# Composing the pool projection and the pool map into one weight, on one core

## The reference

```python
z = rms_norm(h, norm_gain)
proj = z @ w_in                                   # split into q, k, v, g_attn, u_pool, g_pool
o_attn = chunked_window_attention(rotary(q), rotary(k), v, sinks)
u = u_pool.reshape(L, 4, 256)                     # four channel groups
pooled = trailing_mean(u, window=2, 4, 8, 16) - u # one window for each group
mixed = einsum("lgc,gcd->lgd", pooled, w_pool)    # a 256 x 256 map for each group
o_pool = mixed.reshape(L, 1024) * pool_scale
h = h + concat(silu(g_attn) * o_attn, silu(g_pool) * o_pool) @ w_out
y = rms_norm(h, final_norm_gain)[meta dropped]
```

## Time and profile before

| | |
|---|---|
| median of 3 runs | 1375.55 us (1375.39 to 1375.70) |
| span of the profiled execution (first to last instruction) | 1373.9 us |
| mean granted TensorE clock in it | 0.996 |
| PE busy | 1341.3 us, 98% |
| DVE, ACT, POOL busy | 780.0, 536.5, 189.1 us |
| DMA | 102.25 MB, mean 74 GB/s |

### The profile page before, as it was taken

How to read it: one execution, slowest core, us unless ns; L and a number is a source line. 1 busy time by engine, 2 the same in 40 slices (tenths; PEclk the granted TensorE clock), 3 DMA queues, 4 the chain that set the end, 5 groups by cost and what they waited for, 6 DMA issues and landing times.

```text
span 1373.9 us, 18172 instructions
## 1 busy us (share of the span) xinstructions
PE 1341.3 (98%) x6293; PEld 1105.2 (80%) x6293; DVE 780.0 (57%) x1067; ACT 536.5 (39%) x1218; POOL 189.1 (14%) x252
## 2 busy tenths in 40 slices
PE   8999999999999999999999999999999999999997
PEld 6888888787887877888888888887878787788886
DVE  6435355867677674355366435367676868533635
ACT  7222323544444443235344222334444444322433
POOL 1201012111110101000002101031111111000000
PEclk9999999999999999999999999999999999999999
DMA  6011111010101006534433111100101010333442
GB/s 234 32 61 46 46 46 47 8 49 17 50 19 43 26 22 218 161 118 166 143 108 109 44 61 46 46 31 9 61 8 61 8 61 8 107 125 117 151 164 100
DMA packets 29820, 102.25 MB, mean 74 GB/s; under 512 B 3360, under 2 KB 5440, under 8 KB 29792
## 3 DMA queue, kind: packets, MB, share of 16 engines
q1 hardware_dynamic: 22608, 76.03, 16.4%
q0 software_dynamic: 7184, 25.86, 5.6%
HBM read 93.49 MB, written 8.39 MB: 74 GB/s over the span
## 4 chain that ended last, share of the span: by engine, by line
PE 55%; issue 29%; DVE 12%; ACT 1%; POOL 1%; DMA 1%; DVEq 0%; POOLq 0%; SPq 0%; ACTq 0%
PE ps L1148 9%; PE ps L1149 9%; PE ps L1147 8%; PE ps L945 5%; PE ps L946 5%; PE ps L947 5%; DVE wsum L812 3%; DVE stat L799 2%; DVE stat L802 1%; PE ps L1108 1%; PE ps L1067 1%; PE ps L1069 1%; PE ps L1068 1%; PE ps L1093 1%; PE ps L1109 1%
## 5 line engine op out<-in xcount | busy, mean ns | idle before, releaser
L945 PE MATMUL ps<-zh,wsplit 128*128 128x512 f32 x1072 | 421.9, 394 | 0.1
L946 PE MATMUL ps<-zl,wsplit 128*128 128x512 f32 x1072 | 418.3, 390 | 0.0
L947 PE MATMUL ps<-zh,wsplit 128*128 128x512 f32 x1072 | 417.7, 390 | 0.0
L659 DVE TENSOR_TENSOR wsplit<-wraw,wsplit 128x1024 fp32r<-128x1024 f32 (+1 forms) x148 | 203.2, 1373 | 241.2 <-ACT wsplit L437 241.2
L437 ACT ACTIVATE wsplit<-wraw 128x1024 fp32r<-128x1024 f32 (+1 forms) x148 | 146.3, 988 | 265.6 <-PE ps L1149 223.1
L947 PEld LDWEIGHTS ps<-zh,wsplit 128*128 128x128 f32 x1072 | 201.2, 188 | 43.1
L945 PEld LDWEIGHTS ps<-zh,wsplit 128*128 128x128 f32 x1072 | 201.3, 188 | 41.3 <-DVE wsplit L659 0.6
L946 PEld LDWEIGHTS ps<-zl,wsplit 128*128 128x128 f32 x1072 | 201.4, 188 | 39.1
L1149 PE MATMUL ps<-wsplit,gsl 128*128 128x512 f32 x512 | 203.3, 397 | 0.0
L1148 PE MATMUL ps<-wsplit,gsh 128*128 128x512 f32 x512 | 202.7, 396 | 0.0
L1147 PE MATMUL ps<-wsplit,gsh 128*128 128x512 f32 x512 | 199.4, 390 | 2.3 <-POOL gsl L396 2.0
(11 more groups left out here) (156 smaller groups left out, 1588.5 us busy)
## 6 DMA issues: line engine op xcount, KB each, us to landing
wraw<-in_wo SPq DMA_DIRECT2D x64, 512.0 KB, 3.3
wraw<-in_wa SPq DMA_DIRECT2D x36, 512.0 KB, 3.3
wraw<-in_wb SPq DMA_DIRECT2D x32, 512.0 KB, 3.3
rows<-in_x POOLq DMA_DIRECT2D x16, 512.0 KB, 4.3
xr<-in_x POOLq DMA_DIRECT2D x12, 512.0 KB, 3.9
out_y<-rows POOLq DMA_DIRECT2D x8, 512.0 KB, 5.1
xr<-in_x SPq DMA_DIRECT2D x4, 512.0 KB, 6.2
wraw<-in_wp SPq DMA_DIRECT2D x16, 128.0 KB, 2.0
```

The lines of the kernel that those rows point to most:

```text
L659: ve.tensor_tensor(wl[:, slot, 0:size], wraw[:, slot, 0:size], wh[:, slot, 0:size].bitcast(F32), ALU.subtract).then_inc(w_lo, 1)
L945: te.matmul(ps[:, PB[bank], :], w_h, rhs_z(zh, tb, k), start=k == 0, stop=False)
L946: te.matmul(ps[:, PB[bank], :], w_h, rhs_z(zl, tb, k), start=False, stop=False)
L947: last = te.matmul(ps[:, PB[bank], :], w_l, rhs_z(zh, tb, k), start=False, stop=k == KT - 1)
```

## The change

Projection and map are both linear in the channels and pooling acts along the tokens alone, so the map can be applied to the weight. `kernel` now passes the pool columns of `w_in` turned (`wu`, eight blocks of 128 x 1024) and `w_pool` (four blocks of 128 x 512). At the opening of the first half four products are made, one for each group: 48 matmuls of 128 x 256 into PSUM banks 0 to 3 (`product`); ACT copies them to `cout` (`copy_product`), and POOL writes them to the DRAM scratch `wc`. In stage B blocks 0 and 1 are loaded from `wc`; the trailing mean goes to `pooled`, which needs no splitting; a DVE multiplication of 128 x 1024 into the gates stands at the end of chunks 2 and 3. The pool map is gone: `GROUP_BLOCKS` is 4, not 6.

```diff
         def z_bank(h, t):
+            if h == 0 and t < 4:
+                return 4 + 2 * (t % 2)
             return PB[0] if t == 3 else 2 * (t % 3)
+        def composed(eng):
+            for parity in range(2):
+                eng.wait_ge(wc_out[parity], 16 * 2 * NG // 2)
...
 # SP
+            def load_pool(g):
+                if g >= 2:
+                    sp.wait_ge(cp_lo, g - 1)
+                sp.dma_start(cpraw[:, g % 2, :], wp[g]).then_inc(cp_in[g % 2], 16)
+                for ct in range(2):
+                    i = 2 * g + ct
+                    if i >= 4:
+                        sp.wait_ge(cu_lo, i - 3)
+                    sp.dma_start(curaw[:, i % 4, :], wu[g, ct]).then_inc(cu_in[i % 4], 16)
+            load_pool(0)
             sp.dma_start(xr[:, 0, :], x[0, 0]).then_inc(x_first[0], 16)
...
+            load_pool(1)
...
+            load_pool(2)
+            load_pool(3)
             load(0, 0, wa[0], slot_first=True)
...
+                if h == 0:
+                    composed(sp)
...
 # POOL, ahead of the requests for tiles 4 to 7
+            for g in range(NG):
+                pool.wait_ge(cm_sb, 2 * g + 2)
+                for dt in range(2):
+                    gp.dma_start(wc[g, dt], cout[:, g % 2, dt, :]).then_inc(wc_out[g % 2], 16)
...
-                pool.wait_ge(pb_free[1], FREES * (h + 1) - 2 + CREDIT)
+                pool.wait_ge(pb_free[0], FREES * (h + 1) + CREDIT)
                 pool.wait_ge(gs_hi, C_BLOCKS * h + 1)
                 gp.tensor_tensor(gsl[:, 0, :], ...)
...
 # ACT
+            def copy_product(g):
+                if g >= 2:
+                    act.wait_ge(wc_out[g % 2], 16 * 2 * (g // 2))
+                for part in range(2):
+                    act.wait_ge(cm_done, 2 * g + part + 1)
+                    sc.activation(cout[...], ps[:, 2 * part:2 * part + 2, :]..., ACT.Copy).then_inc(cm_sb, 1)
...
-                            sc.activation(plh[:, sub - 1, :], wsum[:, META:META + TOK], ACT.Copy).then_inc(u_hi, 1)
...
-                                    act.wait_ge(u_lo, PT * h + 2 * g + 2)
+                                    act.wait_ge(u_pool, PT * h + 2 * g + 2)
...
+                act.wait_ge(p_gate, PT * (h + 1))
...
 # DVE
+                if h == 0:
+                    composed(dve)
                 rotate((1 + HT) * h, qk[:, :, 0, :])
...
-                            ve.scalar_tensor_tensor(wsum[:, META:META + TOK], ...)
+                            ve.scalar_tensor_tensor(pooled[:, sub - 1, :], ...)
...
-                            ve.tensor_tensor(pll[:, sub - 1, :], ...)
...
+                        if sub >= 2:
+                            i = 2 * g + sub - 2
+                            for tb in range(NTB):
+                                dve.wait_ge(pb_free[tb], FREES * h + HT + i + 1 + CREDIT)
+                            ve.scalar_tensor_tensor(gates[:, HT + i, :], pooled[:, sub - 2, :], stat[...],
+                                                    gates[:, HT + i, :], ALU.mult, ALU.mult).then_inc(p_gate, 1)
...
 # PE
+            def product(g):
+                pe.wait_ge(cp_lo, g + 1)
+                for part in range(2):
+                    if g > 0:
+                        pe.wait_ge(cm_sb, 2 * (g - 1) + part + 1)
+                    for ct in range(2):
+                        if part == 0:
+                            pe.wait_ge(cu_lo, 2 * g + ct + 1)
+                        for k in range(4 * part, 4 * part + 4):
+                            te.matmul(po, u_h, m_h, ...)
+                            te.matmul(po, u_h, m_l, ...)
+                            last = te.matmul(po, u_l, m_h, ...)
+                    last.then_inc(cm_done, 1)
             for h in range(HALVES):
-                for t in range(4):
-                    z_transpose(h, t)
-                if h > 0:
+                if h == 0:
+                    product(0)
+                    z_transpose(0, 0)
+                    z_transpose(0, 1)
+                    product(1)
+                    z_transpose(0, 2)
+                    z_transpose(0, 3)
+                    product(2)
+                    product(3)
+                    pe.wait_ge(cm_sb, 2 * NG - 1)
...
-                    for dt in range(2):                      # the pool map, 24 matmuls
...
```

More of the change, by code:

```diff
@@ L68, with build @@
 USES = A_TILES + B_BLOCKS
-FREES = HT + 4 * NG
-def build(nc, x, meta, wa, wb, wp, wo, gain_n, gain_f, consts, ident_d, rot, rot_meta, out):
+FREES = HT + 2 * NG
+def build(nc, x, meta, wa, wu, wb, wp, wo, gain_n, gain_f, consts, ident_d, rot, rot_meta, out):
+    wc = nc.dram_tensor("wc", (NG, 2, P, KT * P), F32, kind="Internal").ap()
     ctx = ExitStack()
@@ L101, in build @@
         wsplit, _ = place("wsplit", [P, 2, 2, 1024], F32R)
-        plh, pool_at = place("plh", [P, 2, TOK], F32R)
-        pll, _ = place("pll", [P, 2, TOK], F32R)
+        pooled, pool_at = place("pooled", [P, 2, TOK])
+        cursor[0] = pool_at + 16 * TOK
         cos_t = at(pool_at, "cos_t", [P, TOK])
@@ L193, in build @@
         vw_hi, vw_lo = sem("vw_hi"), sem("vw_lo")
-        u_in, u_sum, u_pool, u_hi, u_lo, u_halo = (sem("u_" + n) for n in ("in", "sum", "pool", "hi", "lo", "halo"))
+        u_in, u_sum, u_pool, u_halo = (sem("u_" + n) for n in ("in", "sum", "pool", "halo"))
         gs_hi, gs_lo, gs_first = sem("gs_hi"), sem("gs_lo"), sem("gs_first")
@@ L200, in build @@
         psc_r = sem("psc_r")
+        cu_in = [sem(f"cu_in{i}") for i in range(4)]
+        cp_in = [sem(f"cp_in{i}") for i in range(2)]
+        cu_hi, cu_lo, cp_hi, cp_lo = sem("cu_hi"), sem("cu_lo"), sem("cp_hi"), sem("cp_lo")
+        cm_done, cm_sb = sem("cm_done"), sem("cm_sb")
+        wc_out = [sem(f"wc_out{i}") for i in range(2)]
+        p_gate = sem("p_gate")
         def block_a(h, a):
@@ L405, in _ @@
                     gp.dma_start(gainn[:, :], gain_n).then_inc(gn_in, 16)
+                    pool.wait_ge(p_gate, PT * (h + 1))
                     load_tables(h + 1)
@@ L833, in _ @@
                             ve.tensor_tensor(pr[:, heads], pr[:, heads], rden[:, heads].unsqueeze(2).to_broadcast([P, 4, KEYS]), ALU.mult).then_inc(p_ready, 1)
[L834 to L837 removed]
+                        split_lo(block_b(h, g, sub + 1), (sub + 1) % 2)
                         def gate_tile(tb):
@@ L970, in z_transpose @@
                 pe.wait_ge(z_norm, NTT * h + t + 1)
-                if t == 6:
+                if h == 0 and t in (2, 3):
+                    pe.wait_ge(z_lo, t - 1)
+                elif t == 6:
                     pe.wait_ge(rot_in, 2 * (1 + HT) * h + 1)
@@ L1111, in _ @@
                         te.matmul(ob, vmeta[0:96, :], ptm[0:96, :], start=False, stop=True).then_inc(o_done, 1)
-                    for dt in range(2):
-                        pe.wait_ge(w_lo, block_b(h, g, 4 + dt) + 1)
-                        pe.wait_ge(u_lo, PT * h + 2 * g + 2)
-                        for tb in range(NTB):
-                            pe.wait_ge(pb_free[tb], FREES * h + HT + 4 * g + 2 + dt + CREDIT)
-                            mo = ps[:, PB[tb], :]
-                            for ct in range(2):
-                                m_h, m_l = wh[:, dt, ct * P:ct * P + P], wl[:, dt, ct * P:ct * P + P]
-                                te.matmul(mo, m_h, plh[:, ct, tb * TB:tb * TB + TB], start=ct == 0, stop=False)
-                                te.matmul(mo, m_h, pll[:, ct, tb * TB:tb * TB + TB], start=False, stop=False)
-                                last = te.matmul(mo, m_l, plh[:, ct, tb * TB:tb * TB + TB], start=False, stop=ct == 1)
-                            last.then_inc(pb_done[tb], 1)
                 for tg in range(TG):
@@ L1206 @@
     for g in range(NG):
-        for first in (u0, p0):
-            cols += [np.arange(first + (2 * g + i) * P, first + (2 * g + i + 1) * P) for i in range(2)]
-    wb = tiles(cols).reshape(NG, 4, P, KT * P)
-    wp = np.ascontiguousarray(np.asarray(w_pool)[0].reshape(NG, 2, P, 2, P).transpose(0, 3, 2, 1, 4).reshape(NG, 2, P, 2 * P))
+        cols += [np.arange(p0 + (2 * g + i) * P, p0 + (2 * g + i + 1) * P) for i in range(2)]
+    wb = tiles(cols).reshape(NG, 2, P, KT * P)
+    wu = np.ascontiguousarray(w[:, u0:p0].T.reshape(NG, 2, P, D))
+    wp = np.ascontiguousarray(np.asarray(w_pool)[0].reshape(NG, 2, P, 2 * P).transpose(0, 2, 1, 3).reshape(NG, P, 4 * P))
     rows = np.concatenate(pairs + [HT * P + np.arange(PT * P)])
```

121 lines of the change are left out of this document (83 added, 38 removed).

## The result

The changed kernel takes **1352.9 us** (median of 4 runs, 1352.27 to 1353.39), the kernel before 1375.62 in the same series: ratio 0.983, 95% interval 0.982 to 0.985. The profiled execution has a span of 1351.7 us against 1373.9, 22.2 less, at a mean granted clock of 0.994.

The account below looks back on a forecast made before the run. Outside the opening, PE's instruction list was taken to bound the kernel. Saving 47.5 us in stages B and C and adding 34 in the opening gave -13.5, from 1375.55 to 1362.0 us, range 1354 to 1371.

Parts of the forecast that it names:

- the delay of the opening: Opening, up to the start of stage A: composing the weights and later token tiles add 34 us, bounds 28 to 43.
- the matmuls: Opening, PE: the products' 192 matmuls of 128 x 256 at 0.13 us each take 25.0 us.
- the lower clock: Opening, product 0: after PE idles, about 36 matmuls take twice as long, adding 4.7 us.
- the stall for `ptm`: Stage B, chunk 2: PE's wait for `ptm` goes away, saving 8 x 0.58 = 4.6 us, bounds 0 to 6.
- the stall before stage C: End of each half: without the map as cover, PE stalls about 1.7 instead of 1.16 us, 1.1 lost for both halves.
- Start of `project_k0`: Opening: PE's terms sum to a start at 44.3 us, where it was 17.15, a delay of 27.1 us.
- From there to the first `project`: Opening: token tiles 4 to 7, requested behind the `wc` writes, put the first `project` at 59.3, 32.3 us late.
- The map's 44.0 us: Stage B: removing the pool map's 192 matmuls takes eight times 5.50 us off PE's list.
- The multiplication into the gates: Stage B, end of chunks 2 and 3: DVE's new 1.29 us costs nothing, with 0.45 us of margin left.
- A clock that stays low through the composition: Rival, opening: products run at the lower clock throughout, delay 58 us, time 1386; chance 0.04.
- The late gates: Rival, stage B: gates' multiplication comes 1.2 us late, transposes wait 0.8 in 16 chunks, time 1374.5; chance 0.04.
- the rival with the better hidden opening: Rival, opening: tile 4 lands before `project_k0` ends, PE loses no clock; delay 25, saved 48, about 1352; chance 0.07.

Follow-up runs that it names:

- experiment 4: Changed kernel with the low x high pass of the composition left out, 128 matmuls instead of 192: 1351.29 us.
- experiment 5: Changed kernel with ACT copying product 0 out first and POOL requesting token tiles ahead of the `wc` writes, together: 1344.88 us.
- experiment 6: Changed kernel with the DVE multiplication into the pool gates done twice in chunks 2 and 3, the first into a spare buffer: 1357.1 us.
- experiment 2: Changed kernel with ACT's copy of product 0 placed ahead of the two `zh` copies: 1351.34 us.
- experiment 8: Changed kernel with 8 instead of 20 warm-up matmuls: 1352.6 us.
- experiment 3: Changed kernel with POOL requesting token tiles 4 to 7 between the writes of `wc` instead of behind them all: 1346.07 us.
- experiment 9: Changed kernel with product 0 copied first and token tiles requested between the writes, plus 24 instead of 20 warm-up matmuls: 1345.12 us.
- experiment 1: Changed kernel without the composition: opening of the kernel before, unmapped weights loaded, pool map applied nowhere: 1325.55 us.

## Why the prediction was right in sign and wrong in size

**The step that failed is the delay of the opening: 34 us forecast, 28.4 measured**. It was added up as one line of PE's work, in which the matmuls (25.0, measured 22.75) and the lower clock (4.7, measured 2.5) were sized too high. Beside it the stall for `ptm` was sized 2.5 us too small and the stall before stage C 0.6 too large. The delay stays just inside its bound of 28; the 50.6 saved lie outside theirs of 49. Both went the same way, so the time fell out of the range.

*Start of `project_k0`*, 44.3 forecast, 39.54 measured, term by term:

| term | forecast | measured | difference |
|---|---|---|---|
| start of product 0 | 8.7 | 7.41 | -1.3 |
| 192 matmuls | 25.0 (0.13 each) | 22.75 (0.1185) | -2.3 |
| lower clock | 4.7, in product 0 | 2.5, in product 1 | -2.2 |
| four turned tiles | 3.5 | 3.8 | +0.3 |
| wait for ACT's copy | 2.4 | 3.1 | +0.7 |

The spacing was the choice between half of the map's 0.229 and `project_k0`'s 0.144, which has the last matmul's tail and was the wrong neighbour; half of 0.229 is within 4%. The Trainium skill (TensorE: Matmul & The Clock Gate, Back-to-back issue gap) has 262 cycles for 256 columns as the gap of single matmuls, 0.109 us at 2.4 GHz; the 0.1185 measured in this stream lies 9% above it. The start was early because the two `wu` tiles were there at 4.95 and 6.42, sooner than the 6.5 and 7.8 put for them; in experiment 4 the first of them came 1.5 later, in experiment 5 the second part of product 0 began 2.6 later. The lower clock came, but behind the wait for ACT's copy, and with 26 matmuls at the wider spacing instead of 36. The forecast had taken its return from the earlier trace rows as seven microseconds after work resumed, since no window between 15 and 17.15 was at hand; this one of the kernel before has it back 5.4 us after the start at 10.09:

```profile
15.50:16.00 0.50, 0.00 (x0) 0.00 (x0) 0.50 (x2) 0.50 (x1) 0.25 (x1) 1.00 1.19 164
```

*From there to the first `project`*: 15.0 forecast, 15.65 measured, with the tile requests behind the last write, an idle PE of 5.45 us and a fallen clock, as described; the tile was there at 47.66 rather than 52.4, because everything ahead of its request was earlier and it took 5.6 us, not 5.8. The extra 1.7 for meta statistics and clock was 0.2 (28.2 late at the first `project`, 28.4 at the first scores).

*Stages B and C.* The map's 44.0 us: right; its 5.50 us a group are gone, and 50.3 us in all of both halves. The `ptm` stall was forecast at 4.6 with a bound of 6 and is worth about 7.1, more than its bound: chunks 2 (from first scores to next scores) are 0.67 to 0.72 shorter where 0.58 was taken, and in the second half chunks 1 are 0.37 shorter, 17.31 to 16.94, which stood only in the bound. The start of stage C was forecast 0.55 later per half and is 0.24 later: POOL's subtraction takes 1.27 and 1.26 us in the two halves now and took 1.72 in both before (the earlier trace rows for the first); the row of the second half stands below. 44.0 + 7.1 - 0.5 = 50.6, where 47.5 was forecast.

```profile
1164.68 1.26 POOL L413 TENSOR_TENSOR gsl<-gates_all,gsh 128x512 fp32r<-128x512 f32 x1 [27.24 <-ACT gsh L655]
```

*The multiplication into the gates* was forecast hidden, and it is; the margin was at least twice the one given (experiment 6).

*The rivals.* A clock that stays low through the composition did not come: one drop, 2.5 us. The late gates did not come either. The time is that of the rival with the better hidden opening (1352), but not its mechanism: tile 4 did not land before `project_k0` ended and PE did lose its clock, twice. In the forecast's own terms the delay would have had to be 25; it was 28.4, and the saving 50.6 instead of 48 made up for it.

*What no term of the forecast said*: its sum treats PE's new work, its lower clock and its wait as added one behind the other. Experiments 2, 4 and 8 show that they are exchangeable: with the wait taken away, the matmuls cut by a third, or the lower clock moved elsewhere, the time changed by 1.6, 1.6 and 0.3 us. So a chain outside PE, of landings, splits and copies on ACT and DVE, stands level with PE's own; up to product 1 it is the one that counts, and it begins with the landing of product 1's second `wu` tile (14.48 in the changed kernel, 14.86 to 16.23 in experiments 2, 3, 4, 5 and 9; only in experiment 8, with product 0 slowed, do PE's turned tiles take its place). The forecast had landings only ahead of product 0 and none ahead of product 1. Requesting product 1's `wu` tiles ahead of token tiles 0 and 1, or making the products later, where the DMA engines have room (a share of 0.09 from 60 to 80 us in the changed kernel), was not tried. By contrast the tile requests, which wait on one queue behind work that they don't depend on, were worth their full 6.8.

## What to carry to other kernels

Composing two weights pays when the work removed repeats and the composition is done once, but its price is read where the engines are not full: in the opening, ask which queue the next loads stand on, and put requests ahead of writes that they don't depend on, before counting matmuls. Where an engine waits for another's chain, its lower clock, its wait and its extra work are one price and not three: a term for each overcounts, and an edit to one of them alone gives little. Write that other chain down as a sum of its own, landings included, and take the later of the two. And give every term of a sum a bound on both sides: here the saving of the stall for `ptm` came out above the highest value allowed for it, and the stall before stage C had only one value.

## What the runs showed of the hardware that was not expected

- **Two signs of TensorE's lower clock that disagree.** In experiment 8, 21 matmuls of 256 columns came 0.213 us apart, which is 256 columns at 1.2 GHz, behind 3.79 us of idle, but the windows list the granted clock as 1.00:

```profile
8.00:10.00 2.00, 2.00 (x11) 2.00 (x11) 0.71 (x1) 0.46 (x1) 0.00 (x0) 1.00 1.00 369
...
12.00:14.00 2.00, 2.00 (x19) 2.00 (x18) 1.93 (x4) 0.46 (x3) 0.00 (x0) 1.00 1.03 409
```

  11 matmuls in 2 us stand beside 19 at the full speed. The same holds for the first 14 matmuls of experiment 2 (0.213 apart, windows at 1.00), and in experiment 1 for 24 transposes that took 5.38 us in windows at 1.00, where the kernel before took 5.37 at 0.50. The Trainium skill (TensorE: Matmul & The Clock Gate, Seeing it yourself) warns that recorded clock events can be unreliable; this execution agrees (11 in a window listed at 1.00). The spacing of equal matmuls is the surer reading.
- **Idle time alone does not tell whether the clock falls.** Taken from the spacing of the matmuls behind it: 0.91 us of idle before product 0 left the full clock in the changed kernel, 1.21 in the same place did not in experiment 2, 1.59 did again in experiment 9, and so did 2.12 before product 1 in experiment 8; 3.09 before product 1 brought the lower clock in the changed kernel.
- **The same instruction, 1.26 and 1.72 us.** POOL's subtraction of 128 x 512 before stage C is faster without the map's work before it: 1.26 or 1.27 in both halves of the changed kernel and of experiment 1, 1.72 in both halves before. Which neighbour slowed it was not tried.
- **Landing times under load.** With all DMA engines busy from 4 us on (share 1.0, mostly about 400 GB/s), the first `wu` tile let product 0 begin at 7.4 in one execution and 8.9 in another, and in experiment 5 the second `wu` tile let its second part begin at 11.5. Small differences between versions that change only the opening are therefore read from medians.
